# Stationary weight slices 64 bytes into their slots, an earlier softplus, and the forgetting attention's second half transposed through memory

## The reference, cut to what matters

```python
proj = h @ w_in[l]
a_q, a_f, a_i, a_g, b_q, b_k, b_v, b_f, g_a, g_b = jnp.split(proj, split_points, axis=-1)
y_a = hgrn2_mixer(a_q, a_f, a_i, a_g, lb_table[l], hgrn_norm_w[l]) @ w_up_a[l]
y_b = fox_mixer(b_q, b_k, b_v, b_f + b_fox_f[l]) @ w_up_b[l]
merged = jax.nn.sigmoid(g_a) * y_a + jax.nn.sigmoid(g_b) * y_b
x = x + rms_norm(merged @ w_o[l], norm_mix_post[l])
```

## Time and profile before

| | |
|---|---|
| median of 3 runs | 2555.56 us (2555.49 to 2556.26) |
| the profiled execution's own time | 2555.69 us |
| its span in the trace | 2553.9 us |
| PE busy | 2544.0 us (100% of the span) |
| PE's weight loads busy | 2121.1 us (83%) |
| DVE busy | 1513.2 us (59%) |
| ACT busy | 1248.7 us (49%) |
| mean share of the 16 DMA engines | 64.5% |
| granted TensorE clock | 0.999 of full speed |

### The profile page before, as it was taken

How to read it: one execution, slowest core, us unless ns; L and a number is a source line. 1 busy time by engine, 2 the same in 40 slices (tenths; PEclk the granted TensorE clock), 3 DMA queues, 4 the chain that set the end, 5 groups by cost and what they waited for, 6 DMA issues and landing times.

```text
span 2553.9 us, 33053 instructions
## 1 busy us (share of the span) xinstructions
PE 2544.0 (100%) x13432; PEld 2121.1 (83%) x13432; DVE 1513.2 (59%) x1809; ACT 1248.7 (49%) x1582; POOL 53.6 (2%) x68
## 2 busy tenths in 40 slices
PE   9999999999999999999999999999999999999998
PEld 9878888888888888888888888888888888888887
DVE  6787776555455545576578554556655544555555
ACT  5576655444344434466455454534644444443443
POOL 0150000000000000000000000000000000000000
PEclk9999999999999999999999999999999999999999
DMA  8643557766676666776655566676577666776664
GB/s 302 179 163 120 173 172 248 222 215 211 193 226 209 212 191 214 216 228 216 190 174 165 166 175 194 186 262 197 197 217 227 209 195 209 216 221 195 208 206 149
DMA packets 172840, 515.03 MB, mean 202 GB/s; under 512 B 17104, under 2 KB 48080, under 8 KB 171632
## 3 DMA queue, kind: packets, MB, share of 16 engines
q1 hardware_dynamic: 172544, 512.77, 64.5%
q10 hardware_dynamic: 144, 0.15, 0.0%
HBM read 492.54 MB, written 19.92 MB: 201 GB/s over the span
## 4 chain that ended last, share of the span: by engine, by line
PE 98%; DVE 1%; ACT 1%; issue 0%; DVEq 0%; ACTq 0%
PE ps L516 97%; PE ps L520 1%; ACT W L1152 0%; DVE wlo L1711 0%; DVE W L1711 0%; ACT L1152 0%; ACT whi L1152 0%; DVE W L2381 0%; DVE h L1714 0%; DVE scr L1711 0%; DVEq L2696 0%; ACT scr L1152 0%; ACT sm L1152 0%; DVE RB L1787 0%; DVE W L2564 0%
## 5 line engine op out<-in xcount | busy, mean ns | idle before, releaser
L1711 DVE TENSOR_TENSOR wlo<-raw,whi 128x1024 fp32r<-128x1024 f32 x884 | 1080.3, 1225 | 946.1 <-ACT whi L1152 941.7
L1152 ACT ACTIVATE whi<-raw 128x1024 fp32r<-128x1024 f32 x884 | 933.8, 1059 | 1071.2 <-PE ps L516 1055.5
L516 PE MATMUL ps<-whi,xx 128*128 128x512 f32 x4160 | 1284.9, 390 | 0.0
L516 PEld LDWEIGHTS ps<-whi,xx 128*128 128x128 f32 x4160 | 777.7, 188 | 160.7 <-issue 0.7
L516 PE MATMUL ps<-wlo,xx 128*128 128x512 f32 x2080 | 809.6, 389 | 0.0
L516 PEld LDWEIGHTS ps<-wlo,xx 128*128 128x128 f32 x2080 | 390.4, 188 | 81.5
L516 PE MATMUL ps<-whi,hlo 128*128 128x512 f32 x944 | 368.6, 390 | 0.0
L516 PE MATMUL ps<-whi,hhi 128*128 128x512 f32 x944 | 367.4, 389 | 0.0
L516 PE MATMUL ps<-wlo,hhi 128*128 128x512 f32 x944 | 367.3, 389 | 0.0
L516 PE MATMUL ps<-xx,whi 128*128 128x512 f32 (+1 forms) x1088 | 310.8, 372 | 0.1
L516 PEld LDWEIGHTS ps<-xx,wlo 128*128 128x128 f32 x960 | 180.3, 188 | 37.9 <-DVE wlo L1711 1.2
(11 more groups left out here) (168 smaller groups left out, 916.5 us busy)
## 6 DMA issues: line engine op xcount, KB each, us to landing
raw<-in_gu SPq DMA_DIRECT2D x352, 512.0 KB, 4.3
raw<-in_w_in SPq DMA_DIRECT2D x256, 512.0 KB, 4.1
raw<-in_dn SPq DMA_DIRECT2D x176, 512.0 KB, 4.2
raw<-in_w_out SPq DMA_DIRECT2D x32, 512.0 KB, 3.7
raw<-in_w_up SPq DMA_DIRECT2D x32, 512.0 KB, 4.2
raw<-in_w_o SPq DMA_DIRECT2D x32, 512.0 KB, 4.3
W<-blocks SPq DMA_DIRECT2D x120, 128.0 KB, 2.7
blocks<-W SPq DMA_DIRECT2D x20, 512.0 KB, 6.3
```

Source lines behind the costliest of these rows:

```text
L516: return e.matmul(o, l, r, start=start, stop=stop, skip_group_check=skip)
L1152: return e.activation(o, i, f, **kw)
L1711: return e.tensor_tensor(o, a, b, op)
```

## The change

- whi and wlo get slots of 1056 floats instead of 1024, so slot q starts at 4224 q bytes. In units of kind feat and half the weights are written 16 floats (64 bytes) into the slot and read from there; all others start at the slot's start.
- The pause ahead of the softplus in `gates` is 29 units instead of 35, on ACT and DVE.
- The four chunks o0 to o3 now carry both halves of scr. o2 leaves at the first unit of 2gb2 and o3 five units later; both go through `Hs` and a 32 x 32 block transpose each into the enlarged `Hto`, and `o_tiles` reads them there on ACT and DVE. PE's sixteen transposes are gone. The rows of w_up_b are permuted on the host.
- The wait of SP on `s_tT` ahead of the reload of `h` becomes one on `s_fin`. W, the work area behind these tensors, is 256 floats shorter.

```diff
-        whi = sb("whi", [P, NSPL, 1024], R)
-        wlo = sb("wlo", [P, NSPL, 1024], R)
+        whi = sb("whi", [P, NSPL, 1056], R)
+        wlo = sb("wlo", [P, NSPL, 1056], R)
...
-        Hto = [W_(12288, 1024), W_(13312, 1024)]
+        Hto = [W_(12288 + 1024 * n, 1024) for n in range(4)]
...
-        for n in range(2):
-            chunks[f"o{n}"] = (len(chunks), end["2bf"] + 8 + 8 * n, (s_oa, 2), scr[:, :, n * 512:n * 512 + 512])
+        for n in range(4):
+            chunks[f"o{n}"] = (len(chunks), end["2bf"] + 8 + 8 * n if n < 2 else first["2gb2"] + (-1, 4)[n - 2], (s_oa, 2) if n < 2 else (s_fin, 8),
+                               scr[:, :, n * 512:n * 512 + 512])
...
-            return whi[:, q % NSPL, :], wlo[:, q % NSPL, :]
+            o = 16 if units[q]["item"]["kind"] in ("feat", "half") else 0
+            return whi[:, q % NSPL, o:o + 1024], wlo[:, q % NSPL, o:o + 1024]
...
-            def o_tiles():
-                yield from later(4)
-                for k in range(8, 16, 2):
-                    tiles_T("x", XF["o"] + k, k * 128, scr, (s_fin, 8))
-                    yield
-
...
-            walk(["2gb3"], o_tiles())
+            walk(["2gb3"])
...
-                yield from later(35)
+                yield from later(29)
...
-                    if k < 8:
-                        on.wait_ge(s_bt2, chunks["o1"][0] + 1)
-                        on.wait_ge(s_unit, first["2gb3"] + k // 2 + 1)
-                        for kk in (k, k + 1):
-                            act(xhi[:, kk, :].rearrange("p (ta c) -> p ta c", c=32), by_tiles(Hto[kk // 4])[:, kk % 4],
-                                scale=C("hnw")[:, kk % 4:kk % 4 + 1]).then_inc(s_xhi, 1)
-                    else:
-                        tiles_hi("x", k)
+                    on.wait_ge(s_bt2, chunks["o1" if k < 8 else f"o{k // 4}"][0] + 1)
+                    on.wait_ge(s_unit, first["2gb3"] + k // 2 + 1)
+                    for kk in (k, k + 1):
+                        o, i = xhi[:, kk, :].rearrange("p (ta c) -> p ta c", c=32), by_tiles(Hto[kk // 4])[:, kk % 4]
+                        m = act(o, i, scale=C("hnw")[:, kk % 4:kk % 4 + 1]) if k < 8 else act(o, i)
+                        m.then_inc(s_xhi, 1)
...
-            walk([f"2g{x}{c}" for x in "ab" for c in range(4)][:7], side)
+            walk([f"2g{x}{c}" for x in "ab" for c in range(4)][:6], side)
+            running.append(chain(blocks_o(2, 5), blocks_o(3, 5)))
+            walk(["2gb2"], side)
...
-                    on.wait_ge(s_tT, 14)
+                    on.wait_ge(s_fin, 8)
...
-        "w_up": np.stack([pack(by_blocks(a["w_up_a_2"][0], range(2)), 4), pack(a["w_up_b_2"][0], 4)]),
+        "w_up": np.stack([pack(by_blocks(a["w_up_a_2"][0], range(2)), 4), pack(by_blocks(a["w_up_b_2"][0], range(2)), 4)]),
```

More of the change, by code:

```diff
@@ L584, in first_unit @@
                 banks = pair_of(i)
-                wh = whi[:, 0, :].rearrange("p (k n) -> p k n", n=CH)
-                wl = wlo[:, 0, :].rearrange("p (k n) -> p k n", n=CH)
+                wh, wl = (w.rearrange("p (k n) -> p k n", n=CH) for w in slot(0))
                 on.wait_ge(s_hi, 1)
@@ L2512, in o_tiles @@
                 for k in range(0, 16, 2):
[L2513 to L2520, removed]
+                    tiles["x"] += 2
+                    on.wait_ge(s_xhi, tiles["x"])
+                    for kk in (k, k + 1):
+                        o, i = (ap.rearrange("p (ta c) -> p ta c", c=32) for ap in (xlo[:, kk, :], xhi[:, kk, :].bitcast(F)))
+                        b = by_tiles(Hto[kk // 4])[:, kk % 4]
+                        m = stt(o, b, C("hnw")[:, kk % 4:kk % 4 + 1], i, MUL, SUB) if k < 8 else tt(o, b, i, SUB)
+                        m.then_inc(s_xlo, 1)
                     yield
```

## The result

The changed kernel takes 2587.18 us (median of 4 runs, 2586.35 to 2587.84) against 2555.52 us for the one before on the same chip: 1.0123 times, 95% interval 1.0105 to 1.0141. It is 31.7 us slower. Forecast were 2552.1 us in 2544 to 2556, with 0.08 for slower. Both the size and the sign are wrong.

What follows compares the result with a forecast made beforehand. PE's stream of matmuls was taken as the bound; transposes 1.9, softplus 0.5 and the 64 bytes 1.1 sum to 3.5 us off, from a median of 2555.56 us to 2552.1 us, range 2544 to 2556.

Steps and rivals of the forecast that it cites:

- The slots of tok weights: Tok matmuls, whose weight slots move by 0 to 384 bytes: no cost, bounded by 1.5 us on 9,072 matmuls.
- the 3.4 ns between 116.6 and 120.0 ns: Rates of 256-column matmuls in thin and feat; as an upward step on 2048 feat and half matmuls, a loss bound of 7 us.
- the sign to look for: In the profile after: the prediction is wrong if a tok unit, 2.722 us, moves by as little as 0.01 us.
- The softplus: Near 250 us, the three steps six units earlier remove PE's idle 0.48 us: -0.5 us, between 0 and -0.5.
- the work they move beside is ACT's again, three units ahead of PE: Softplus at its earlier place: the work beside it runs three units ahead of PE; worst case of the term 0.
- The 64 bytes: Feat and half stationary weights: the shift frees 3.1 ns in each of 375 half groups, -1.1 us; gain bound -20 us.
- the sum of the parts at their old rates: Half group: 2 x 226.8 + 2 x 120.0 = 693.6 ns against 696.7 recorded; the shift frees the 3.1 ns.
- the address as such moves nothing between them: Stationary loads in thin (512-byte multiples, 116.6 ns) and cmp (480-byte steps, 116.4 ns): address makes no difference between them.
- Rival 3: Feat and half: shifted stationary reads get slower, 3.7 ns on each of 2048 matmuls, 2560.7 us; chance 0.08.
- Taken as the prediction took them: The skill's pages, for feat and half weights: the 64-byte shift gains 0, and the sum is 1.1 us less.
- The transposes: Sixteen PE transposes between 1637 and 1647 us go and nothing replaces them on PE: -1.9 us.
- Rival 4: 2gb2 and 2gb3: SP's wait for the new chunks makes raw loads late, 2.5 us each, 2557.1 us; chance 0.03.

Runs made afterwards that it cites:

- Experiment 1: The kernel before with slots of 1056 floats and all weights at their slot's start, nothing else: 2587.9 us, 1.0127 times the kernel before.
- experiment 2: The changed kernel with slots of 1088 floats instead of 1056, the 64 bytes for feat and half kept: 2555.42 us, 1.000 times the kernel before.
- experiment 7: The kernel before with only the Exp of a_log moved right behind the softplus's own exponential: 2555.17 us against 2555.64, 0.9998 times.
- the third of the last: The kernel before plus transposes through memory, slots of 1088 floats, feat 64 and half 192 bytes in, a_log's exponential early, softplus unmoved: 2550.29 us, 0.9977 times.
- experiment 3: The kernel before with ACT's and DVE's softplus parts six units sooner and nothing else: 2560.47 us, 1.0019 times.
- experiment 5: The map: kernel before with transposes through memory, slots of 1088 floats, tok weights 0 to 240 bytes in, each half item its own offset: 2598.79 us, one run.
- experiment 6: The map again, with xx 128 bytes further on and offsets only for tok items that read xx: 2588.47 us, one run.
- experiment 9: The kernel before with the softplus six units sooner, but DVE's steps behind the Ln six units later again: 2557.43 us, 1.0008 times.

## Why the prediction was wrong

**The slots of tok weights.** This is the step that failed: "So 0, bounded by 0.16 ns either way on 9,072 matmuls: 1.5 us". The runs show about 3.6 ns a matmul: (657.72 - 647.38) / 2856 = 3.62 ns, and times 9,072 32.8 us. Experiment 1 has the 32.5 us by itself and experiment 2 takes them back. The step had the right count and looked at the right addresses, but its rows could not carry it. Xx and hhi both lie on multiples of 256 bytes from the slots, a difference at which nothing is lost; no row of the trace had a slot 128 bytes off. The bound was then the spread of two equal cases and not of the unknown one. The prediction had a wider step at hand, the 3.4 ns between 116.6 and 120.0 ns, and used it for the 2048 matmuls that the edit aims at; on the 9,072 that it moves in passing it would have made a bound of 31 us. One sign stood in the trace unread: cmp's mean of 116.4 ns is made of distances of 112 to 120 ns that come in the same order in both units, while its stationary slices step through 480 bytes. That this is the same effect is not shown. The last paragraph of the prediction did name the sign to look for, a tok unit off by 0.01 us; they are off by 0.01 to 0.02 and by 0.07.

**The softplus**: forecast -0.5 us, "between 0 (another late step takes the wait) and -0.5"; measured +5.0 alone. The stall at 250 went as forecast (0.5 us in experiment 7, 0.7 in the third of the last). What failed is the reasoning "the work they move beside is ACT's again, three units ahead of PE". It counted the split and not what stands behind it on DVE: the copy and the product at 228.29 that PE reads without a margin of units, only 0.95 us. Nor did it count the waits that move along: the exponential's wait for DVE (1.88 us in experiment 3) stands in front of ACT's split. With the Ln's table load of 1.28 us and DVE's steps, 2.4 us, all of it is ahead of that product. The wait alone is no harm: in the kernel before the same exponential waits 4.32 us, until 241.82, in front of a split too, and PE loses nothing, since no product with so small a margin stands behind it. A worst case of 0 would have needed the row at 228.29.

**The 64 bytes**: forecast 3.1 ns a half group, 696.7 to 693.6; measured 693 in the slots 64 bytes off and 691 in those 192 off. The size was right, but not by its reason, and so by luck: the forecast took the sum of the parts at their old rates as what a group falls to, while in the map a group runs at 689 ns at 192 bytes, under that sum, and at 704 and 707 at 16 and 160, over it, and the parts' own rate moved as well. Feat was forecast at 0 and measured at 2.2 to 6.7 ns a matmul, 0.8 to 2.6 us. That "the address as such moves nothing between them", taken from thin and cmp, does not carry over to feat, half or tok. Rival 3, the only one that decides on the side where the time fell, put its loss on the 2048 stationary reads and gave it 2560.7 us; these got faster. The loss came through the moving reads, which no rival had.

The Trainium skill says of PE's accesses that they "never wait on anyone" (SBUF — State Buffer, section SBUF: two separate sides). It also gives the weights and the moving operand independent read ports (TensorE: Matmul & The Clock Gate, section Step-by-step: what each phase is for). Taken as the prediction took them, the two leave experiments 1, 5 and 6 no slower than the kernel before. They are 32.5, 43 and 33 us slower; the measurement decides.

**The transposes**: forecast -1.9 us, measured -1.98. Rival 4 can be dropped. SP did wait 10.3 us in four, more than the 2.5 us each that it allowed for at the longest (3.7), the DMA share rose to 0.85, and no wait of PE came of it. The two transposes more on DVE didn't reach PE either.

**What stays open.** Why the difference of the two starts matters is not shown; the curve has no simple form (good at 0 and 240, fair at 64, worst at 208), and no run tells the difference of the starts from their sum. In the changed kernel and in experiment 1 the slots on a multiple of 256 run at 228.0 ns, 1.3 above the map's value for 0, while their neighbours at 128 run at 233.0 as in the map. In the changed kernel's trace all of that stands in such a unit's first three distances (231.7, 232.5 and 230.9 ns on average), and the rest are at 226.7 to 227.1: what a unit catches from the slower one ahead of it is gone after three matmuls. How it is carried over wasn't tried. And feat's 113.3 or 117.8 ns at the same offsets is unexplained, and with it most of the 2.2 us by which the runs of the last kernel differ.

## What to carry to other kernels

When a buffer's stride changes, count every instruction that reads it and not those that the edit is for, and bound their cost by a row at the new offset; rows at the old one bound nothing. Where one engine is the whole time, a padding that keeps both operands' starts a multiple of 256 bytes apart cost nothing here, and one of 128 bytes on every second slot cost 1.3%. Before a small step is moved onto an engine, look for the next result of that engine that the critical engine reads. The step has to fit into the margin of that result, here 0.95 us; the three units by which the weight splits run ahead are not its margin.

## What the hardware showed unasked

- The start-to-start time of an fp32r matmul of 512 columns depends on how its two operands' starts lie to each other modulo 256 bytes (experiment 5; weights moving, activations stationary): 226.7 ns at 0, 226.6 at 240, 228.9 at 64, 232.9 at 128, 234.6 at 208. It is not the moving operand's own address: with the stationary operand moved by 128 bytes the curve moved by 128 (experiment 6).
- For matmuls whose weights are stationary the best of the tried distances is not 0: a half group takes 696 ns at 0, 693 at 64 and 689 at 192, and 704 at 16.
- In a unit at 0 that follows one at 128 the loss lingers for three matmuls: distances of 231 to 232.5 ns in place of 226.7 (changed kernel, slots 0 and 2).
- After an idle time of 3.96 to 3.99 us PE ran at a granted clock of 0.50, the 1.2 GHz level, for a few us, which cost 1.1 us in the changed kernel and 2.0 in experiment 3; after one of 1.98 us (experiment 9) it ran on at 1.00, the 2.4 GHz level.
